# Asking for the experts' down-projection weights from ScalarE's hardware DMA queue instead of SyncE's

## What is computed

```
gates = top-1 of 4 groups, then top-2 of its 8 experts, per token
for e in range(32):
    he = silu(xt @ w_gate[e]) * (xt @ w_up[e])     # 1024 -> 512, twice
    out = out + gates[:, e] * (he @ w_down[e])     # 512 -> 1024
```

## Time and profile before

| | |
|---|---|
| median of 3 runs | 1394.44 us (1393.88 to 1397.04) |
| profiled execution | 1395.1 us; span in the profile 1393.2 us |
| granted TensorE clock, mean | 0.956 |
| TensorE busy | 1243.3 us (89%) |
| VectorE, ScalarE busy | 280.8 us (20%), 205.9 us (15%) |
| DMA | 458.78 MB, mean 329 GB/s, 79.7% of the 16 engines' span on one queue |
| experts of layer 0, units 0 to 11 | about 295 to 759 us |
| experts of layer 1, units 0 to 11 | about 935 to 1382 us |

### The profile page before, as it was taken

How to read it: one execution, slowest core, us unless ns; L and a number is a source line. 1 busy time by engine, 2 the same in 40 slices (tenths; PEclk the granted TensorE clock), 3 DMA queues, 4 the chain that set the end, 5 groups by cost and what they waited for, 6 DMA issues and landing times. The chain is left out here.

```text
span 1393.2 us, 15227 instructions
## 1 busy us (share of the span) xinstructions
PE 1243.3 (89%) x6130; PEld 627.0 (45%) x6130; DVE 280.8 (20%) x679; ACT 205.9 (15%) x490; POOL 34.0 (2%) x42
## 2 busy tenths in 40 slices
PE   6999999989999999769686998999999999757685
PEld 6875876454444445313232566454444443322221
DVE  3542453041111110100002156031111111100001
ACT  3124233120000000000002246130000000000001
POOL 0001210000000000000000011000000000000000
PEclk9999999999999999879899999999999999887897
DMA  9543307559999997999999722439999999999994
GB/s 378 188 159 121 122 0 287 226 220 425 425 425 420 426 425 318 427 425 426 427 426 388 299 103 91 182 139 417 423 419 427 425 427 427 425 427 426 427 427 177
DMA packets 78282, 458.78 MB, mean 329 GB/s; under 512 B 7040, under 2 KB 7040, under 8 KB 28928
## 3 DMA queue, kind: packets, MB, share of 16 engines
q1 hardware_dynamic: 78208, 457.75, 79.7%
HBM read 456.67 MB, written 1.05 MB: 329 GB/s over the span
## 5 line engine op out<-in xcount | busy, mean ns | idle before, releaser
L1407 PE MATMUL bank<-own,e_xg 128*64 128x512 f32 (+1 forms) x1272 | 273.9, 642 | 38.8 <-DMA late<-in_w_up 9.6
L1407 PE MATMUL bank<-late,e_xg 128*32 128x512 f32 (+1 forms) x648 | 167.8, 656 | 15.2 <-DMA late<-in_w_gate 7.3
L1407 PEld LDWEIGHTS bank<-own,e_xg 128*64 128x64 f32 (+1 forms) x1272 | 79.4, 130 | 203.4 <-issue 203.3
L1416 PE MATMUL bank<-own,e_turned 128*64 128x512 f32 (+1 forms) x592 | 129.2, 675 | 33.2 <-DMA own<-in_w_down 19.9
L1299 DVE TENSOR_TENSOR e_hid<-e_silu,bank 128x512 f32<-128x512 f32 x24 | 25.6, 1068 | 507.9 <-ACT e_silu L1350 507.9
L1416 PE MATMUL bank<-late,e_turned 128*64 128x512 f32 (+1 forms) x392 | 91.1, 680 | 16.8 <-DMA late<-in_w_down 7.6
L1382 PEld LDWEIGHTS bank<-e_pick,xs 128*128 128x128 f32 x768 | 93.4, 199 | 22.4 <-issue 18.7
L1382 PE MATMUL bank<-e_pick,xs 128*128 128x128 f32 x768 | 99.8, 286 | 3.5 <-DVE e_pick L1241 3.5
L1350 ACT ACTIVATE e_silu<-bank 128x512 f32<-128x512 f32 x24 | 14.3, 598 | 545.3 <-PE bank L1407 545.3
L1407 PEld LDWEIGHTS bank<-late,e_xg 128*32 128x32 f32 (+1 forms) x648 | 46.6, 132 | 96.9 <-issue 96.8
L1399 PE MATMUL bank<-e_y,e_gates_T 128*128 128x512 f32 x192 | 86.5, 593 | 1.4 <-ACT e_gates_T L1358 1.4
(11 more groups left out here) (341 smaller groups left out, 1120.6 us busy)
## 6 DMA issues: line engine op xcount, KB each, us to landing
own<-in_w_gate SPq DMA_DIRECT2D x83, 1024.0 KB, 12.5
own<-in_w_up SPq DMA_DIRECT2D x76, 1024.0 KB, 10.6
own<-in_w_down SPq DMA_DIRECT2D x74, 1024.0 KB, 12.4
late<-in_w_down SPq DMA_DIRECT2D x49, 1024.0 KB, 11.3
late<-in_w_up SPq DMA_DIRECT2D x41, 1024.0 KB, 11.4
late<-in_w_gate SPq DMA_DIRECT2D x40, 1024.0 KB, 12.7
own<-in_a_in_w SPq DMA_DIRECT2D x18, 1024.0 KB, 12.4
extra<-in_w_up SPq DMA_DIRECT2D x11, 1024.0 KB, 12.0
```

Source lines behind the costliest of these rows:

```text
L1407: ins = pe.matmul(bank[q * T:(q + 1) * T, :], self.xg[:, at:at + T], cut(tile(q), k=4)[:, k, :], start=(half == 0 and k == 0), stop=(half ...
L1416: ins = pe.matmul(self.b_down[out][q * T:(q + 1) * T, :], self.turned[:, at:at + T], cut(tile(q), j=2)[:, j, 512 * out:512 * out + 512], s ...
```

## The change

The loop on SyncE leaves out the down jobs. ScalarE asks for them, on the hardware queue that it has itself, at two places in its work on a unit u: behind the two copies `turned`, for down jobs whose slot was last held by a gate, up or `mem_w_kv` granule of unit u; and behind the copy of the gates, for those whose slot was last held by a down granule of unit u. Before each it waits for the same semaphore count as SyncE did. It also loads the order of the groups (`quads`) at the start of each layer's block. Slots, places in SBUF, sizes and TensorE's waits are unchanged, and so are the first 18 jobs of a layer. There are 348 expert granules asked for inside the two blocks; of these 120 down granules go to ScalarE.

```diff
+    @staticmethod
+    def is_down(job):
+        return job[0] == "expert" and job[3] == "down"
+
+    def down_loads(self, act, u, after, quad):
+        for job in expert_jobs(self.layer)[FIRST_JOBS:]:
+            prev = before(job)
+            unit, stage = (SIDE[prev[1]], "up") if prev[0] == "mem" else (prev[2], "down" if self.is_down(prev) else "up")
+            if self.is_down(job) and (unit, stage) == (u, after):
+                act.wait_ge(*self.released(prev))
+                self.c.load_job(act, job, self.job_source(job, quad))
...
@@ sync block
                 for n, job in enumerate(jobs):
-                    if n < FIRST_JOBS:
+                    if n < FIRST_JOBS or self.is_down(job):
                         continue
...
@@ scalar block
+                quad = self.quads(act)
                 for u in range(NU):
...
                     for half in range(2):
                         act.activation(self.turned[:, 256 * half:256 * half + 256], self.b_turn[:, 256 * half:256 * half + 256],
                                        ACT.Copy).then_inc(s["turned_ready"], 1)
+                    self.down_loads(act, u, "up", quad)
                     act.wait_ge(s["down_done"], u * 2 + 2)
                     act.activation(self.y[0][:, :], self.b_down[0][:, :], ACT.Copy).then_inc(s["y_ready"], 1)
                     act.wait_ge(s["gates_turned"], u + 1)
                     act.activation(self.gates_T[:, :], self.b_turn[:, 0:SEQ], ACT.Copy).then_inc(s["gates_ready"], 1)
+                    self.down_loads(act, u, "down", quad)
```

## The result

| | before | after |
|---|---|---|
| median of four runs, us | 1394.18 | 1491.06 |
| lowest to highest, us | 1393.88 to 1397.04 | 1490.45 to 1496.67 |
| span of the profiled execution, us | 1393.2 | 1489.7 |

The ratio is 1.070, with a 95% interval of 1.068 to 1.072. The change costs 96.9 us, where 83 were forecast.

What follows compares the result with a forecast made beforehand. The stream of weights was taken to pace the narrow units, so late down granules there add 82.7 us to the profiled 1395.1 us, 1477.8, for a median of 1477 us; range 1420 to 1515 us, about 0.8.

Steps and rivals of the forecast that it cites:

- part 2: Narrow units: down granules asked for only when TensorE wants them; a unit takes 30.3 + 2.46 N us, 13.9 more with side product.
- N: Narrow units: granules moved from the late ask to the last down granule, 2.46 us each; taken as 16 or 12.
- equal turns: Narrow units: the two queues are served alternately, N 16 or 12; 1455 to 1500 us, chance 0.62.
- rival 1: Narrow units: down granules pass the others, N 8 or 6; 1421 us, chance 0.17.
- rival 2: Narrow units: down granules stand behind all of SyncE's, N 18 or 16; 1526 us, chance 0.13 with anything slower.
- Part 1: Wide units: down granules asked for late but covered by 7 us; cost 0, bounded by 0 and 4 us per layer.
- keep_busy: Unit 11: no gate or up granule is waited for any more, so this 4.56 us filler stands on the path each time.
- the +1.0 and 0 of that unit: Unit 11: forecast change of +1.0 us in layer 0 and 0 in layer 1.
- the dry stretch of some 20 us: Unit 11: sign that the DMA engines run dry for some 20 us.
- Part 3: ScalarE's issues and its `quads` loads: cost 0, at most 7.4 us for both layers if the loads stood in the open.
- Rival 3: Narrow units: SyncE runs ahead and the hole at 537 to 547 us closes, at most 8.1 us; 1386 us, chance 0.05.

## Why the prediction was right, and where not

**The term that decides, part 2**, came out as written. Unit time was forecast as 17.0 + 2.4 + 2.46 N + 10.9 us, plus 13.9 for a side product; half 1 of the down step starts 10.9 us before the end. From its start, N can be read back:

| unit | start, us | down half 1 starts | N, worked out | N, forecast |
|---|---|---|---|---|
| layer 0, 8 | 529.20 | 601.08 | (71.9 - 33.3) / 2.46 = 15.7 | 16 |
| 9 | 612.19 | 662.98 | (50.8 - 19.4) / 2.46 = 12.8 | 12 |
| 10 | 673.87 | 746.69 | (72.8 - 33.3) / 2.46 = 16.1 | 16 |
| layer 1, 8 | 1230.73 | 1287.50 | (56.8 - 19.4) / 2.46 = 15.2 | 12 |

The first three say equal turns (rival 1 needed 8 or 6, rival 2 18 or 16). The landings of unit 8 in layer 0 say it more directly: one down granule each 4.9 us, where rival 1 had one each 2.46 us, and the first 8.8 us after its ask, where rival 2 had it after more than 15. For unit 9 the turns read 12.8, an error of 2 us; in layer 1, units 9 and 10 together are 3.6 us over the forecast. The Trainium skill ("DMA: Bandwidth & Descriptors", section "Queues, rings and completion order") says that an engine goes round the queues that have work; by that N was 16 or 12, and now the trace agrees, with 15.7, 12.8 and 16.1. The same page's section "Issuing engines are not separate DMA queues" says that several issuing engines save issue time alone; of the bytes moved the trace agrees (427 GB/s). But it was not all that a second queue did here: the granules landed in another order, for 7 to 27 us.

**Part 1 is the step that failed.** It said that the hole of the first wide unit "only eats into the lead", and took 0. The hole was there (5.0 us where the wide units alone are moved), the wide units kept 29.5 us and none of them waited, all as written. But in layer 1 the lead isn't slack: the stream is the bound of everything that follows, and each granule by which it is ahead at the start of the narrow units shortens unit 8. Its 35.7 us before, against 58.5 of the next one, was that lead. In layer 0 the same hole is free, since there the stream stands idle anyway from 537 to 547 us, with its slots full: that idle time shrank from 8.4 to 2.4 us when the wide units' hole came ahead of it. In terms of the sum, unit 8 of layer 1 had 17.0 us from its start to the end of `e_turned`; the first ask there comes after 16.5 us with the wide units on SyncE, after 23.0 with all on ScalarE. The last row of the table (N 15.2) is this error and not one of the turns: from the first ask to the start of half 1 it is 1287.50 - 1253.71 = 33.8 us, where 2.4 + 29.5 = 31.9 were forecast, and that gives N = 12.8, as in unit 9 of layer 0. The bound given, 4 us per layer, was too low as well: the hole alone is 5.0 us, and with the wait of 3.71 us and the lower clock behind it, the wide units' asks cost 7.0 us in unit 8.

**keep_busy** on the path of unit 11, three times 4.56 us: right, shown by leaving it out. So was the +1.0 and 0 of that unit, and the dry stretch of some 20 us in it. In layer 1:

```profile
1432.00:1454.00 22.00, 17.93 (x100) 6.06 (x92) 1.04 (x1) 1.26 (x3) 0.00 (x0) 1.00 0.05 10
```

**Part 3, nothing for the issues:** right. An issue takes 0.34 us on ScalarE, and its next copy comes 46.61 us later anyway, held by TensorE. Where the issues do delay a copy, by 1.8 us, the time is still 13 us below that of the kernel after.

**The rivals.** None came true. The asks made early came to 1421.9 us, the figure of rival 1, but by chance and by another road: there, too, the queues take turns. Rival 3 (faster, the hole at 537 us closes) went the other way: that hole grew from 8 to 22 x 0.43 = 9.5 us, as nothing asked for fills slots that aren't free. What closes it is the order of TensorE's work.

The forecast was 1477 us and the median 1491. Of the 14 us, 7.8 are unit 8 of layer 1, 1.7 unit 9 of layer 0, and 3.6 the units 9 and 10 of layer 1.

## What to carry to other kernels

Before a load moves to another engine's instruction stream, look at what stands ahead of it there: the moment of the ask was worth 69 to 90 us here, the queue and the engine 7 to 27. Where one stream is the bound, count the lead with which it enters the bound stretch as time, even if no unit waits near the place where it is lost. And here a single queue kept the order of need; two queues on the same DMA engines delivered in turns, so that an urgent granule landed each 4.9 us instead of each 2.46.

## What the runs showed of the hardware that was not expected

Issuing never held ScalarE. On SyncE's queue, in the kernel before, an issue took 2.05 us in the middle and up to 6.2 when many were outstanding; on ScalarE's it took 0.34 us, with eight asked for at once and the engines full, and 0.68 at most over all 120. With the down granules gone, no ask for an expert's granule on SyncE's queue took more than 1.24 us either. Two transfers that alternate cost no bandwidth: 427 GB/s with both queues at work (559 to 601 us), 425 and 426 with one. TensorE's granted clock was 0.60 on average from 559 to 601 us, in which it was busy for 6.34 us, and the two halves of the down step in unit 8 took 5.97 and 5.52 us instead of 3.64. The sum had this in half 1 (5.34 us), and in half 0 it is hidden, as half 1 waits for granules.
